# A two-layer hybrid decoder trunk on one core: the steady feed-forward chunks as straight code instead of engine loops

## What is computed

```python
for l in range(DEPTH):                       # DEPTH = 2, x is (1, 256, 2048) float32
    h = _rmsnorm(x, attn_norm[l])
    proj = jnp.einsum('bsd,de->bse', h, w_in[l])
    ...
    mixed = jnp.concatenate([o_diff, o_gla, o_mla], axis=-1)
    x = x + jnp.einsum('bse,ed->bsd', mixed, w_out[l])

    h2 = _rmsnorm(x, ffn_norm[l])
    ff = jax.nn.silu(jnp.einsum('bsd,df->bsf', h2, w_gate[l])) * jnp.einsum('bsd,df->bsf', h2, w_up[l])
    x = x + jnp.einsum('bsf,fd->bsd', ff, w_down[l])
return _rmsnorm(x, final_norm)
```

## Time and profile before

| | |
|---|---|
| median of 3 runs | 2185.74 us (2184.55 to 2187.57) |
| the profiled execution | 2186.89 us, its span 2185.1 us |
| granted TensorE clock, mean | 0.998 |
| busy: TensorE matmuls, weight loads | 2163.6 us (99%), 1843.1 us (84%) |
| busy: VectorE, ScalarE, GpSimd | 1715.3 us (78%), 1083.2 us (50%), 24.0 us (1%) |
| read from HBM | 399.54 MB, 184 GB/s over the span |

### The profile page before, as it was taken

How to read it: one execution, slowest core, us unless ns; L and a number is a source line. 1 busy time by engine, 2 the same in 40 slices (tenths; PEclk the granted TensorE clock), 3 DMA queues, 4 the chain that set the end, 5 groups by cost and what they waited for, 6 DMA issues and landing times.

```text
span 2185.1 us, 27181 instructions
## 1 busy us (share of the span) xinstructions
PE 2163.6 (99%) x10826; PEld 1843.1 (84%) x10826; DVE 1715.3 (78%) x1934; ACT 1083.2 (50%) x1142; POOL 24.0 (1%) x24
## 2 busy tenths in 40 slices
PE   8999999999999999999999999999999999999998
PEld 7899988888888888888888999888878888888886
DVE  5576774788898888889755867747888898888886
ACT  5454543554554545545443645435545454445443
POOL 0000000000000000000000000000000000000000
PEclk9999999999999999999999999999999999999999
DMA  7544455555655565565555434555555655665664
GB/s 249 181 133 131 140 178 185 181 193 194 204 198 192 193 207 194 194 207 194 192 180 166 146 111 161 174 177 192 193 192 196 206 193 193 199 204 192 201 202 154
DMA packets 221103, 402.77 MB, mean 184 GB/s; under 512 B 13376, under 2 KB 53600, under 8 KB 220896
## 3 DMA queue, kind: packets, MB, share of 16 engines
q1 hardware_dynamic: 220304, 400.90, 55.8%
q10 hardware_dynamic: 720, 0.78, 0.1%
HBM read 399.54 MB, written 2.10 MB: 184 GB/s over the span
## 4 chain that ended last, share of the span: by engine, by line
PE 95%; DMA 2%; DVE 1%; ACT 1%; issue 1%; SPq 0%; POOLq 0%; POOL 0%; ACTq 0%; DVEq 0%
PE bank L1014 19%; PE bank L1016 19%; PE bank L1015 19%; PE bank L693 10%; PE bank L695 10%; PE bank L694 10%; PE bank L653 2%; DMA stage<-in_w_in 1%; PE bank L818 1%; DMA stage<-in_w_down 1%; ACT w_hi L1177 1%; PE bank L759 0%; PE bank L882 0%; DVE w_lo L1532 0%; PE bank L870 0%
## 5 line engine op out<-in xcount | busy, mean ns | idle before, releaser
L1532 DVE TENSOR_TENSOR w_lo<-stage,w_hi 128x2048 fp32r<-128x2048 f32 (+4 forms) x319 | 679.4, 2132 | 272.6 <-ACT w_hi L1177 272.2
L1177 ACT ACTIVATE w_hi<-stage 128x2048 fp32r<-128x2048 f32 (+4 forms) x319 | 569.3, 1787 | 393.5 <-DMA stage<-in_w_down 192.1
L693 PE MATMUL bank<-w_hi,xt_hi 128*128 128x512 f32 (+4 forms) x1048 | 376.8, 360 | 6.6 <-DVE xt_lo L1593 4.2
L695 PE MATMUL bank<-w_hi,xt_lo 128*128 128x512 f32 (+4 forms) x1048 | 369.5, 353 | 0.0
L694 PE MATMUL bank<-w_lo,xt_hi 128*128 128x512 f32 (+4 forms) x1048 | 369.3, 352 | 0.0
L1014 PE MATMUL bank<-w_hi,xt_hi 128*128 128x512 f32 x812 | 316.4, 390 | 0.0
L1016 PE MATMUL bank<-w_hi,xt_lo 128*128 128x512 f32 x812 | 315.9, 389 | 0.0
L1015 PE MATMUL bank<-w_lo,xt_hi 128*128 128x512 f32 x812 | 315.9, 389 | 0.0
L1014 PE MATMUL bank<-w_hi,f_hi 128*128 128x512 f32 x696 | 273.2, 392 | 2.4 <-DVE kept L2016 1.5
L1016 PE MATMUL bank<-w_hi,f_lo 128*128 128x512 f32 x696 | 271.0, 389 | 0.0
L1015 PE MATMUL bank<-w_lo,f_hi 128*128 128x512 f32 x696 | 271.0, 389 | 0.0
(11 more groups left out here) (258 smaller groups left out, 2819.2 us busy)
## 6 DMA issues: line engine op xcount, KB each, us to landing
stage<-in_w_gate SPq DMA_DIRECT2D x176, 512.0 KB, 3.8
stage<-in_w_up SPq DMA_DIRECT2D x176, 512.0 KB, 4.7
stage<-in_w_down SPq DMA_DIRECT2D x174, 512.0 KB, 4.6
stage<-in_w_in SPq DMA_DIRECT2D x96, 384.0 KB, 3.7
stage<-in_w_out SPq DMA_DIRECT2D x64, 512.0 KB, 4.4
stage<-in_w_in SPq DMA_DIRECT2D x54, 512.0 KB, 4.7
stage<-in_w_in SPq DMA_DIRECT2D x16, 320.0 KB, 3.4
stage<-in_w_q_b SPq DMA_DIRECT2D x12, 384.0 KB, 3.8
```

Of the source, the lines that this page charges most:

```text
L693: pe.matmul(acc, a, wh[:, i, :], start=first and i == 0, stop=False)
L695: mm = pe.matmul(acc, b, wh[:, i, :], start=False, stop=last and i == len(kts) - 1)
L1177: act.activation(w_hi[s][:, 0:kts * cols], stage[s][:, 0:kts * cols], ACT.Copy).then_inc(hi_made[s], 1)
L1532: vec.tensor_tensor(w_lo[s][:, 0:kts * cols], stage[s][:, 0:kts * cols], w_hi[s][:, 0:kts * cols].bitcast(F32), ALU.subtract).then_inc(lo_ ...
```

## The change

On TensorE, ScalarE and VectorE the engine loop over the steady chunks becomes a loop of the program that writes the kernel, so that the same code is written out eight times in each layer, with constants in place of registers. Nothing else differs.

```diff
@@ -1140,7 +1140,7 @@
                     down(0, c, U_SECOND + 8)
                 added(0, 2)
                 ff_turn(1, TURN_BANKS)
-                with pe.Fori(LOOP_FROM, FF_CHUNKS - 1) as f:
+                for f in range(LOOP_FROM, FF_CHUNKS - 1):
                     gate_up_sets(f, U_BODY, 3 * f - 3 * LOOP_FROM)
                     for c in range(4):
                         down(f - 1, c, U_BODY + 8, 3 * f - 3 * LOOP_FROM)
@@ -1455,7 +1455,7 @@
-                with act.Fori(LOOP_FROM, FF_CHUNKS - 1) as f:
+                for f in range(LOOP_FROM, FF_CHUNKS - 1):
@@ -2107,7 +2107,7 @@
-                with vec.Fori(LOOP_FROM, FF_CHUNKS - 1) as f:
+                for f in range(LOOP_FROM, FF_CHUNKS - 1):
```

## The result

| | before | after |
|---|---|---|
| median | 2185.18 us (2184.27 to 2187.57, 7 runs) | 2193.13 us (2191.93 to 2194.8, 7 runs) |
| the profiled execution, its span | 2186.89, 2185.1 us | 2192.52, 2190.7 us |

The ratio is 1.0033 (95% interval 1.0023 to 1.0042): written out, the kernel takes 0.33% longer, about 8 us. (The seven runs of before are the three shown earlier and four more, hence a median 0.56 lower.) The forecast had said 2188.7, which is 4.4 us or 0.2% too low. The time is inside the range, 2184.8 to 2193.2, at its upper edge; the sum of +3.0 us was less than half of what came.

What follows compares the result with a forecast made beforehand. TensorE's stream of matmuls, 95% of the chain, was taken to bound the kernel. Loop 0, wait +3.0, vanished hit -1.5 and new fetch meetings +1.5 made +3.0 on 2185.74: 2188.7 us, range 2184.8 to 2193.2.

Steps and rivals of the forecast that it cites:

- The loop itself: Register additions, branches and wait-limit arithmetic at each turn on three engines: removing them gains 0, covered by the sequencer's lead.
- The wait at the first down product: Written out, `combined` stands first with other waits behind it, delaying each chunk's first down product: +3.0 us over 16 chunks.
- The charge of 0.19: Cost per chunk of the reordered waits at the first down product: 0.21 less 0.02 to spare, for 16 chunks.
- The fetches: TensorE's instruction fetches meeting loads: layer 1's existing hit vanishes, -1.5 us; new meetings in written-out chunks cost +1.5 us.
- The long stop: TensorE's 1.47 us stop on L2016 in layer 1's first looped chunk, laid to a fetch: expected to vanish, -1.5 us.
- 2.4 meetings: Expected number of fetches falling into the vulnerable load over 16 chunks, at a mean of 0.6 us each: +1.5 us.
- 0 + 3.0 - 1.5 + 1.5: The forecast's sum: loop machinery, wait at the first down product, vanished layer 1 hit, new fetch meetings; +3.0 us.
- the ring: TensorE frees the buffer, load lands (4.3 us), ScalarE rounds, VectorE subtracts, then L2016 and the product; claimed without slack.
- The faster one: Rival: loop machinery does cost, so the chunk's 0.31 us falls below 0.1 and layer 1's hit goes: -5.2, 2180.5; chance 0.05.
- Nothing, or almost: Rival: ring's load lands earlier or the waits hide under the previous product; layer 1's hit goes: 2184.2 to 2185.7; chance 0.16.
- The third: Rival: fetches repeatedly meet loads, five hits of 1.47 us: +8.8, 2194.5; chance 0.22, including ScalarE's or VectorE's fetches.
- what would show it: Signs in chunks formerly looping: L2016 to product 0.94 to 0.95, stops about 0.2 to 0.3 us, windows 63.8 instead of 63.64.

Runs made afterwards that it cites:

- av_only: The kernel before with only ScalarE's and VectorE's loops written out, TensorE's loop kept: 2187.30 us, ratio to before 1.0006.
- e1: The changed kernel with the waits of the first down product reordered so that the matmul itself holds `combined`: 2190.74 us, ratio to before 1.0021.
- b1: The kernel before, loops kept, with the first down product's waits reordered to put `combined` in the matmul; layer 1's loop came out otherwise: 2187.17 us, ratio 1.0005.
- loops_tail_of_waits: The kernel before, loops kept, with 8000 always satisfied wait instructions behind TensorE's last matmul: chunk 63.89 us against 63.63; total time not comparable.
- before_pad_512k: The kernel before with one more input of 512 KB that nothing reads, declared ahead of the others: 2186.37 us, ratio to before 0.9999.
- pe_only: The kernel before with only TensorE's loops written out, ScalarE's and VectorE's kept: 2192.88 us, ratio to before 1.0039.

## Why the prediction came out as it did

**The loop itself, 0: right.** The spacing at a chunk's end is unchanged (0.80 and 0.31), and av_only moves nothing. The Trainium skill, Runtime: NRT & Kernel Launch, section "Instruction fetch mechanics", has a taken branch stall when its target isn't in the fetched window; the prediction worked out from this a gain at each turn. No packet of TensorE's moves while the loop of layer 0 turns, and no run here shows such a gain.

**The wait at the first down product, +3.0: right in mechanism and nearly in size.** 0.94 instead of 0.74 in every chunk, 0.74 again when the order is changed back (e1), 0.92 with the order changed in a loop (b1, layer 1). In time: 2.1 to 3.0 us by the medians, as said at e1; 0.13 us a chunk by the median periods (64.04 and 63.91) and 0.21 by the means, so 2.1 to 3.4 us over sixteen. The charge of 0.19 is inside that.

**The fetches, -1.5 + 1.5: right in size, partly by luck.** The long stop went. Against it, chunks with something extra came: of the fourteen periods of after twelve are 63.92 to 64.17 and two are 64.79 and 64.67, 1.4 us over their median together. The first of them in the trace: one packet of TensorE's instructions while a half-gate, half-up buffer is loading (transfers from 683 to 685 us), ScalarE waiting for that load, and TensorE's stop behind what ScalarE and then VectorE (`f_lo`) do after it, in after:

```profile
q8 instruction: 1, 0.02, 3.1%
```

```profile
689.10 1.92 ACT L1177 ACTIVATE w_hi<-stage 128x2048 fp32r<-128x2048 f32 x1 [4.45 <-DMA stage<-in_w_up]
```

```profile
692.27 0.39 PE L1016 MATMUL bank<-sums_hi,xt_lo 128*128 128x512 f32 x1
692.95 0.50 PE L1014 MATMUL bank<-w_hi,xt_hi 128*128 128x512 f32 x1 [0.29 <-DVE f_lo L1941]
```

The meeting wasn't at the load of w_down that the prediction had taken for the only vulnerable one, and neither was the second: in the chunk of 64.67 a packet at 2052.6 us falls into a gate-and-up load that takes 5.95 us instead of 4.70. On the load that the prediction had in mind, no packet falls into the middle in any of the sixteen chunks (one overlaps its last half microsecond), so its 2.4 meetings agree with the runs in number only. That the packets caused these stops was read from the trace, not tried.

**The step that failed is the sum itself: "0 + 3.0 - 1.5 + 1.5".** It had no term for the price of the code's mere presence, and "Their bytes are nothing (0.5 MB beside 400)" was taken as the end of the matter. It isn't: with a longer TensorE program w_down loads land 0.25 us later, all through. The prediction had the ring right ("being tied to TensorE's own progress, it does not catch up"), so this passes through whole: 0.26 us a chunk in loops_tail_of_waits, 0.29 from before to e1, and 0.07 less in both against before_pad_512k. Over sixteen chunks that is 16 x 0.26 = 4.2 us, or 3.0 with 0.19. The sum as the runs have it, for the profiled executions: 2.1 to 3.4 for the waits, 3.0 to 4.2 for the landings, -1.4 for the long stop (65.29 less 63.63 is 1.66, and 64.31 still has 0.27 over the median), +1.4 for the two odd chunks: 5.1 to 7.6. The trace has +6.5 over the sixteen: 14 x 0.50 = 7.0, +0.5 in layer 0's first (64.10 against 63.59), -1.0 in layer 1's first. Outside the sixteen, after is 0.9 shorter, which is of the size by which identical stretches differ from run to run (the first 497.3 us of before are 496.1 in after, 494.8 in pe_only). That makes the 5.6 between the two profiled executions; the medians lie 7.95 apart because the profiled one of before is 1.7 above its median and that of after 0.6 below.

**The rivals.** The faster one needed the chunk's 0.31 us to shrink; it didn't. "Nothing, or almost" needed slack in the ring, and there is next to none: after's stop of 0.46 us is the two delays of 0.20 and 0.24 and before's 0.02. The third, clearly slower at 2194.5, came within 1.4 us of the measured time for the wrong reason: it wanted five fetches that stop TensorE 1.47 us each, where two small ones came and a steady 0.26 a chunk did the rest. The half of the forecast's "what would show it" that spoke of windows of 63.8 and stops of 0.2 to 0.3 us failed at once (64.10 and 0.46), while every mark of the wait's mechanism was there; a window that is off by 0.3 beside a delay that is exact should be read as a second cause, not as a mis-sized first one.

**What stays open.** How the length of one engine's program slows the loads of two tensors. What the runs have: w_down and w_out (rows of 8 KB, 2048 floats) are slower, gate and up (rows of 22 KB) aren't, at 4.65 to 4.73 in all kernels, short and long; it holds from the first loads of w_out on, with or without packets in flight; w_down takes 4.71, 4.87, 5.03 and 4.95 us at 54, 63, 70 and 86 packets; inputs shifted by 36 KB, 512 KB or 32 MB change nothing. A placement of the tensors or of the program in memory that depends on the program's size would fit, but no run shows it. Whether ScalarE's or VectorE's program could do the same at a larger size wasn't tried.

## What to carry to other kernels

Where several semaphores are waited for at a critical instruction, see that the one that arrives last is held by that instruction itself, and look in the built order for it, since an edit of the source can come out differently in two copies of the same code: here it was worth 0.2 us each time, 2 to 3 us in all. This loop, whose turn showed no gap on the engine, had nothing to give back, and the longer program made some loads land 0.25 us later in a ring that has no slack. Before a loop like it is unrolled, such a term is to be charged, and the cheap test is to append dead instructions at the end and compare load times and periods in the part that hasn't changed.
